# First recurrence of a two-block layer stack: where its values are turned, where its state products stand, and its low score levels issued in pairs

## The chip, the cores and the metric

The kernel runs on one core of a Trainium2 chip. The metric is the device time of one execution in microseconds (us), median of several executions; less is better. A core has a matrix engine (PE in the profile), a vector engine (DVE), an activation engine (ACT), a general engine (POOL) and an engine that issues the loads here (SP). Each runs its own list of instructions in order; they wait for each other through semaphores. PE writes only to PSUM, eight banks of 128 partitions x 512 float32.

## The reference, cut to what matters

The program is an attention layer, a gated recurrence with its projections, and a second block (a delta rule, a gated linear attention), for 2048 tokens of width 1024 in float32. The change is within the first recurrence alone, with 8 heads whose keys and values are 128 wide:

```
proj = h @ w_in;  q, f, i, z = split(proj)      # 4 x 1024 columns
q = silu(q);  k = 1 - exp(log_f);  v = i        # log_f: a log gate made of f
b = cumsum(log_f)                               # in a chunk
scores[t, s] = sum_k q[t] * exp(b[t] - b[s]) * k[s]        (s <= t)
o = (q * exp(b)) @ S + scores @ v
S = S * exp(b_last) + (k * exp(b_last - b)).T @ v
o = rmsnorm(o) * gnorm_w * silu(z)
```

## The kernel before, in words

`recurrence` (line 1017 of the profile's file) keeps features on the partitions and works in 32 units: a unit is one head and 512 tokens (four chunks of 128). Units 2n and 2n+1 are one visit: one head, two neighbouring groups of tokens, with the same weights. The visits pass the 8 heads over the first 1024 tokens and then over the second.

**Front of a unit.** Four projections, in the order q, z, f, v, each with eight steps (one per 128 rows of the contraction). A step is `product` (lines 191 to 195): three matmuls 128x128x512 of rounded parts, high by high, high by low, low by high. So a front has 32 steps and 96 matmuls. ACT then makes tanh of q, z and f and a logarithm (thq, thz, thf, lg), DVE makes q, z, k and the running sum b (lines 182, 178, 1423), and ACT takes v out of PSUM (step "v"). PE turns v, four 128x128 transposes ("vt", line 1138), and ACT copies the result to v_at. POOL makes the differences for score level 0 ("d", lines 1356 and 1357), ACT their exponential ("dx"), DVE its two halves e1 and e2 (lines 1437 and 1438); I call these two E0.

**Back of a unit.** Scores inside a chunk are made by halving. PE makes the diagonal ("diag", line 1152), then for levels 0 to 6 a product of keys with queries (steps "l0" to "l6"; line 1174 for levels 0 to 5, whose outputs are 64 partitions high, line 1170 for level 6). For each level from 1 on POOL makes differences, ACT exponentials ("dx1" ...), DVE two halves ("lev1" here for the two instructions of level 1, and so on); after PE, DVE merges the result into the scores (line 1466, "s0" ...). Then PE turns the keys ("kt", line 1184), DVE copies them out (line 1471), PE multiplies turned keys by turned values ("ds", line 1195), DVE carries four states (line 182, "st0" to "st3"), and PE makes the outputs in two halves ("o", lines 1205 and 1209). ACT squares the output ("sq"), PE sums over features ("norm", line 1219), ACT takes logarithm and exponential ("ln", "rs"), and DVE scales twice (line 1487 "on", line 182 "out").

**The order of the work** is written out by hand. Front and back are generators on each engine; `in_turn` runs front(u+1) and back(u) together, and `merge` (line 156) always advances the generator that is behind by its share of steps. The two counts are the numbers of `yield` in each:

```
merge((front(u + 1) if u + 1 < UN else None, 36), (back(u), 23))
```

A `yield` with nothing before it therefore only moves what follows later against the other generator. Of such a merge I say that its front is odd or even, by the number u+1.

**Weights.** SP loads the four weight blocks of the next visit (512 KB each, line 1097) as soon as the last products with the old ones are done. ACT rounds a block (128x1024, line 187) and POOL subtracts (line 1345). The code names them by the projection behind which they stand (`piece_due`): in fronts of odd units w(z), w(f), w(v) behind the projections z, f and v (they carry the weights of q, z and f of the next visit), in fronts of even units w(q), with the weights of v.

**PSUM.** The front has a ring of four banks, the back another, each taken in PE's order; who takes a bank waits until the one of four takes before has been read.

**Heads that begin.** In fronts of units 0, 1, 16 and 17 ACT and DVE also make the high and low parts of h (eight steps, line 1414), for which PE's q products wait.

Of the kernel before, what the change touches and what calls it, by code (L numbers as in the profile page):

```python
# [14 lines left out]
P = 128  # L15
# [19 lines left out]
LEVELS = 7  # L35
# [981 lines left out]
def recurrence(k):  # L1017
# [36 lines left out]
    set_a = k.steps("bounds_exp", "l0", "l1")  # L1054
    Fpe = k.steps("front_products", "q", "z", "f", "v", "vt")
    Fa = k.steps("front_scalar", "thq", "thz", "thf", "lg", "v", "dx", "vt")
    Fv = k.steps("front_vector", "q", "z", "k", "b", "e1", "e2")
    Fp = k.steps("front_pool", "d")
    Bpe = k.steps("back_products", "diag", *(f"l{l}" for l in range(LEVELS)), "kt", "ds", "o", "norm")
    Ba = k.steps("back_scalar", *(f"dx{l}" for l in range(1, 6)), "dx6", "eb", "dk", "sq", "ln", "rs")  # L1060
    Bv = k.steps("back_vector", "e1_1", "e2_1", "diag", *(x for l in range(5) for x in (f"e1_{l + 2}", f"e2_{l + 2}", f"s{l}")),
# [3 lines left out]
    def taken_front(kind, u):  # L1065
        at = {"q": (Fv, "q"), "z": (Fv, "z"), "f": (Fa, "thf"), "v": (Fa, "v"), "vt": (Fa, "vt")}
        s, name = at[kind]
        return s.by(name, u)

    def taken_back(kind, u):  # L1070
        at = {"diag": (Bv, "diag"), "kt": (Bv, "kt"), "ds": (Bv, "st3"), "o": (Bv, "on"), "norm": (Ba, "ln")}
        s, name = at[kind] if kind in at else (Bv, kind)
        return s.by(name, u)

    def in_turn(front, back):
        run(front(0))
        for u in range(UN):
            merge((front(u + 1) if u + 1 < UN else None, 36), (back(u), 23))

# [25 lines left out]
    def on_pe():  # L1105
# [16 lines left out]
        def front(u):  # L1122
            yield from project(0, "q", u)
            yield
            yield from project(3, "z", u)
            yield
            yield from project(1, "f", u)
            for _ in range(4):
                yield
            yield from project(2, "v", u)  # L1130
            yield
            b, before = fb.take("vt", u)
            pe.wait_ge(*Fa.by("v", u))
            if before is not None:
                pe.wait_ge(*taken_front(*before))
            for j in range(4):
                sl = slice(j * P, (j + 1) * P)
                ins = pe.transpose(b[:, sl], th(u, 2)[:, sl], k.c("ident"))
            ins.then_inc(*Fpe.did("vt"))
            yield  # L1140

        def back(u):
# [10 lines left out]
            ins.then_inc(*Bpe.did("diag"))  # L1153
            yield
            for l in range(LEVELS):
                H = 1 << l
                if l <= 5:
                    yield
                e = e0_at if l == 0 else e_of(u, l - 1)
                b, before = kb.take(f"s{l}", u)  # L1160
                if l == 0:
                    pe.wait_ge(*Fv.by("e2", u))
                else:
                    pe.wait_ge(*Bv.by(f"e2_{l}", u))
                if before is not None:
                    pe.wait_ge(*taken_back(*before))
                for i in range(4 if H == CH else 8):
                    if H == CH:
                        sl = slice(i * P, (i + 1) * P)
                        ins = pe.matmul(b[:, i * CH:(i + 1) * CH], e[:, sl], view(e[:, sl], H)[:, :, 1, :],  # L1170
                                        start=True, stop=True)
                    else:
                        own, sl = slice(i % 2 * CH, (i % 2 + 1) * CH), slice(i * CH, (i + 1) * CH)
                        ins = pe.matmul(b[own, i * CH // 2:(i + 1) * CH // 2], e[:, sl], view(e[:, sl], H)[:, :, 1, :],  # L1174
                                        start=True, stop=True)
                ins.then_inc(*Bpe.did(f"l{l}"))
                yield
            b, before = kb.take("kt", u)
# [6 lines left out]
            ins.then_inc(*Bpe.did("kt"))  # L1185
            yield
            yield
            b, before = kb.take("ds", u)
            pe.wait_ge(*Bv.by("kt", u))
            pe.wait_ge(*Fa.by("vt", u))  # L1190
            if before is not None:
# [4 lines left out]
            ins.then_inc(*Bpe.did("ds"))  # L1196
            yield
            b, before = kb.take("o", u)
# [48 lines left out]
    def on_act():  # L1247
# [10 lines left out]
        def front(u):  # L1258
            h, g = unit(u)
            if h == 0:  # L1260
                if g == 0:
                    a.wait_ge(*set_v.by("sel"))
                if u:
                    a.wait_ge(*Fpe.by("v", u - 1))
                for c in range(KC):
                    act(a, hi_of(g)[:, c, :], k.hT[:, c, cols(g)], ACT.Copy).then_inc(*h_a.did("hi"))
            yield from project("q", u)
            yield
            yield from project("z", u)
            yield  # L1270
            yield from project("f", u)
            a.wait_ge(*Fpe.by("z", u))
            if u:
                a.wait_ge(*Fv.by("z", u - 1))
            k.tanh(th(u, 0), fb.at("q", u), scale=0.5).then_inc(*Fa.did("thq"))
            if u:
                a.wait_ge(*Fpe.by("vt", u - 1))
            k.tanh(th(u, 1), fb.at("z", u), scale=0.5).then_inc(*Fa.did("thz"))
            a.wait_ge(*Fpe.by("f", u))
            if u:  # L1280
                a.wait_ge(*Fv.by("b", u - 1))
            else:
                a.wait_ge(*set_v.by("ab"))
            k.tanh(tf_at, fb.at("f", u), scale=0.5).then_inc(*Fa.did("thf"))
            a.wait_ge(*Fa.by("thf", u))
            k.ln(lg_at, tf_at, bias=ab[:, h:h + 1], scale=bb[:, h:h + 1]).then_inc(*Fa.did("lg"))
            for _ in range(4):
                yield
            yield from project("v", u)
            a.wait_ge(*Fv.by("q", u))  # L1290
            a.wait_ge(*Fpe.by("v", u))
            act(a, th(u, 2), fb.at("v", u), ACT.Copy).then_inc(*Fa.did("v"))
            a.wait_ge(*Fp.by("d", u))
            act(a, e0_at, e0_at, ACT.Exp).then_inc(*Fa.did("dx"))
            yield
            a.wait_ge(*Fpe.by("vt", u))
            act(a, v_at[u % 2], fb.at("vt", u), ACT.Copy).then_inc(*Fa.did("vt"))
            yield
# [5 lines left out]
        def back(u):  # L1304
            h, g = unit(u)
            level(u, 1)
            yield
            yield
            for l in range(LEVELS):
                if l + 2 < LEVELS:  # L1310
                    level(u, l + 2)
                    yield
                elif l + 2 == LEVELS:
                    if u:
                        a.wait_ge(*Bv.by("st3", u - 1))
                    act(a, eb_at, b_at[u % 2], ACT.Exp).then_inc(*Ba.did("eb"))
                    a.wait_ge(*Bp.by("dk", u))
                    act(a, d_of(u, 6), d_of(u, 6), ACT.Exp).then_inc(*Ba.did("dk"))
                    yield
                yield  # L1320
            for _ in range(5):
                yield
# [18 lines left out]
    def on_pool():  # L1341
# [17 lines left out]
        def front(u):  # L1359
# [4 lines left out]
            yield from project("f", u)  # L1364
            for _ in range(4):
                yield
            yield from project("v", u)
# [3 lines left out]
            differences(u, 0, e0_at).then_inc(*Fp.did("d"))  # L1371
            yield
            yield
# [12 lines left out]
        def back(u):  # L1386
            level(u, 1)
            yield
            yield
            for l in range(LEVELS):  # L1390
                if l + 2 < LEVELS:
# [7 lines left out]
                yield  # L1399
            for _ in range(8):  # L1400
                yield
# [5 lines left out]
    def on_dve():  # L1407
        def front(u):
# [7 lines left out]
            for _ in range(7 + 1 + 7 + 1 + 7 + 3):  # L1416
# [7 lines left out]
                                 op0=ALU.mult, op1=ALU.add).then_inc(*Fv.did("b"))  # L1424
            yield
            for _ in range(7):
                yield
            v.wait_ge(*Fa.by("dx", u))
            v.wait_ge(*Fv.by("k", u))
            halves(u, 0, e0_at, e0_at, Fv, "e1", "e2")  # L1430
            yield
            yield
# [11 lines left out]
        def back(u):  # L1444
# [4 lines left out]
            v.wait_ge(*Bpe.by("diag", u))  # L1449
            v.tensor_tensor(v4(sc_at), v4(kb.at("diag", u)), bc(k.c("ident"), 1, 4), ALU.mult).then_inc(*Bv.did("diag"))  # L1450
            yield
            for l in range(LEVELS):
# [18 lines left out]
            v.tensor_copy(kt_at, kb.at("kt", u)).then_inc(*Bv.did("kt"))  # L1471
            yield
            yield
            bs = kb.at("ds", u)
            v.wait_ge(*Bpe.by("ds", u))
            for j in range(4):
# [5 lines left out]
                else:  # L1482
                    stt(v, new, old, eb_at[:, j * P + P - 1:j * P + P], bs[:, sl], ALU.mult, ALU.add).then_inc(*Bv.did(f"st{j}"))
            for _ in range(5):
                yield
# [1295 lines left out]
```

## Time and profile before

| | us |
|---|---|
| median of 3 executions | 4064.3 |
| lowest, highest | 4064.14, 4067.91 |
| the profiled execution | 4071.8 |
| its span in the profile | 4070.5 |

The profile holds the start and duration of each instruction. A matmul's record is longer than the distance to the next one, since matmuls overlap: two products stand 0.23 us apart and have 0.39 us each. So I read costs on PE from the distance of starts. In a timeline a row's number in brackets is how long the engine had stood idle, and who released it; a row with x16 holds sixteen records; a float32 matmul leaves two.

### The profile page before, as it was taken

How to read it: one execution, taken by the hardware profiler on the slowest of the kernel's cores; microseconds unless marked ns; L12 is line 12 of the kernel's file. 1: busy time of each engine (PE TensorE's matmuls, PEld its weight loads, DVE VectorE, ACT ScalarE, POOL GpSimd, SP SyncE). 2: the span in 40 equal slices, each digit the busy share in tenths (PEclk: the TensorE clock that was granted, in tenths of full speed). 3: DMA queues.
4: the chain of work that ended last, by engine and by line, in shares of the span. 5: the costliest groups of instructions: out<-in, count | busy, mean ns of one | idle time of the engine just before them, and what ended most of it. 6: DMA issues, size and time to landing. Idle time of an engine off the chain costs nothing.

```text
span 4070.5 us, 78395 instructions
## 1 busy us (share of the span) xinstructions
PE 3683.8 (90%) x32928; PEld 2775.6 (68%) x32928; DVE 2043.2 (50%) x4568; ACT 1582.1 (39%) x2978; POOL 1124.8 (28%) x1214
## 2 busy tenths in 40 slices
PE   7999979897999998999997979999999996888889
PEld 4555548685777776777775856777776774777767
DVE  4655652344555555555554434656666664233222
ACT  2444441222344444443443324444444442344332
POOL 0000001132344443444432323222222320333232
PEclk9999989898999999999997989999999997999999
DMA  3000000122010110110101332111111113222132
GB/s 120 27 1 1 1 11 26 73 88 95 22 37 27 31 33 22 33 31 27 37 21 68 127 125 53 39 38 38 44 39 38 38 29 120 63 63 63 44 110 90
DMA packets 220093, 202.64 MB, mean 50 GB/s; under 512 B 7072, under 2 KB 191840, under 8 KB 219744
## 3 DMA queue, kind: packets, MB, share of 16 engines
q1 hardware_dynamic: 219744, 197.62, 15.5%
q8 instruction: 264, 4.33, 0.4%
q14 instruction: 85, 0.70, 0.1%
HBM read 164.04 MB, written 33.55 MB: 49 GB/s over the span
## 4 chain that ended last, share of the span: by engine, by line
PE 77%; DVE 10%; ACT 7%; issue 3%; DMA 2%; POOL 2%; SPq 1%; ACTq 0%; DVEq 0%; POOLq 0%
PE bank L193 18%; PE bank L195 16%; PE bank L194 16%; PE bank L447 4%; ACT arena L187 3%; PE bank L1174 3%; PE bank L2234 2%; DVE arena L685 2%; PE bank L2245 1%; ACT L277 1%; DVE arena L178 1%; PE bank L487 1%; ACT arena L188 1%; DVE arena L182 1%; PE bank L311 1%
## 5 line engine op out<-in xcount | busy, mean ns | idle before, releaser
L194 PE MATMUL bank<-hT_cut,arena_cut 128*128 128x512 f32 x2080 | 830.1, 399 | 0.0
L187 ACT ACTIVATE arena<-bank 128x512 f32<-128x512 f32 (+1 forms) x584 | 311.6, 570 | 745.2 <-PE bank L195 550.6
L193 PE MATMUL bank<-hT_cut,arena_cut 128*128 128x512 f32 x1112 | 515.7, 464 | 38.3 <-POOL arena_cut L1870 27.9
L187 ACT ACTIVATE arena<-arena 128x512 f32<-128x512 f32 (+3 forms) x690 | 359.4, 549 | 298.4 <-POOL arena L1357 222.4
L194 PEld LDWEIGHTS bank<-hT_cut,arena_cut 128*128 128x128 f32 x2080 | 401.5, 193 | 81.4 <-issue 19.0
L195 PE MATMUL bank<-hT_cut,arena_cut 128*128 128x512 f32 x1112 | 444.6, 400 | 0.0
L193 PE MATMUL bank<-arena_cut,hT_cut 128*128 128x512 f32 (+1 forms) x960 | 363.9, 379 | 61.7 <-POOL oT_cut L949 61.7
L188 ACT ACTIVATE arena<-arena 128x256 f32<-128x256 f32 (+2 forms) x336 | 210.1, 626 | 512.7 <-DVE arena L177 277.9
L193 PE MATMUL bank<-oT_cut,arena_cut 128*128 128x512 f32 x712 | 318.8, 448 | 56.9 <-POOL arena_cut L2503 23.0
L194 PE MATMUL bank<-arena_cut,hT_cut 128*128 128x512 f32 (+1 forms) x960 | 359.8, 375 | 0.0
L2503 POOL TENSOR_TENSOR arena_cut<-arena,arena_cut 128x256 fp32r<-128x256 f32 x272 | 224.3, 854 | 472.5 <-ACT arena_cut L187 472.4
L195 PE MATMUL bank<-arena_cut,oT_cut 128*128 128x512 f32 x768 | 306.1, 399 | 0.0
L447 PE MATMUL bank<-arena,hT 128*128 128x512 f32 (+1 forms) x768 | 297.0, 531 | 1.7 <-DVE arena L634 1.6
L193 PEld LDWEIGHTS bank<-hT_cut,arena_cut 128*128 128x128 f32 x1112 | 214.1, 193 | 106.0 <-ACT arena L187 30.3
L195 PE MATMUL bank<-oT_cut,arena_cut 128*128 128x512 f32 x712 | 283.6, 398 | 0.0
L1437 DVE TENSOR_TENSOR arena<-arena 128x256 f32<-128x256 f32 x224 | 149.4, 667 | 260.8 <-ACT arena L187 260.8
L187 ACT ACTIVATE arena<-bank,arena 128x512 f32<-128x512 f32 (+1 forms) x176 | 93.2, 561 | 468.2 <-PE bank L195 442.5
L187 ACT ACTIVATE arena_cut<-arena 128x1024 fp32r<-128x1024 f32 (+1 forms) x204 | 220.5, 1085 | 132.3 <-DMA arena<-in_rec_w_in 75.9
L1356 POOL TENSOR_TENSOR arena<-arena 128x256 f32<-128x256 f32 x224 | 146.7, 655 | 384.3 <-DVE arena L1423 254.5
L193 PEld LDWEIGHTS bank<-arena_cut,hT_cut 128*128 128x128 f32 x960 | 182.5, 190 | 99.2 <-issue 65.0
L195 PEld LDWEIGHTS bank<-hT_cut,arena_cut 128*128 128x128 f32 x1112 | 213.7, 192 | 50.3
L1345 POOL TENSOR_TENSOR arena_cut<-arena,arena_cut 128x1024 fp32r<-128x1024 f32 x64 | 155.4, 2430 | 302.4 <-ACT arena_cut L187 302.4
(237 smaller groups left out, 7079.3 us busy)
## 6 DMA issues: line engine op xcount, KB each, us to landing
arena<-in_w_in SPq DMA_DIRECT2D x100, 512.0 KB, 3.8
arena<-in_rec_w_in SPq DMA_DIRECT2D x64, 512.0 KB, 4.1
x_after<-arena SPq DMA_DIRECT2D x32, 512.0 KB, 2.6
arena<-x_after SPq DMA_DIRECT2D x32, 512.0 KB, 4.2
oT<-in_x SPq DMA_DIRECT2D x16, 512.0 KB, 3.4
arena<-in_x SPq DMA_DIRECT2D x16, 512.0 KB, 3.4
h_after<-hT SPq DMA_DIRECT2D x4, 2048.0 KB, 7.7
hT<-h_after SPq DMA_DIRECT2D x4, 2048.0 KB, 16.7
```

Of the source, the lines that this page charges most:

```text
L187: return e.activation(out, a, f, bias=bias, scale=scale)
L188: return e.activation(out, a, f, bias=bias, scale=scale, accum_out=accum)
L193: pe.matmul(out, a[0], b[0], start=start, stop=False)
L194: pe.matmul(out, a[0], b[1], start=False, stop=False)
L195: return pe.matmul(out, a[1], b[0], start=False, stop=stop)
L447: ins = pe.matmul(b[:, 0:n], k.hT[:, c, t * P:(t + 1) * P], wq[:, c, c0:c0 + n], start=(c == 0), stop=(c == KC - 1))
L685: m = v.tensor_tensor_reduce(out=prob4(u)[:, h, lo:], in0=banks.at(f"s{par}", u)[:, j * 256 + lo:(j + 1) * 256], in1=band[:, lo:], scale=H ...
L1174: ins = pe.matmul(b[own, i * CH // 2:(i + 1) * CH // 2], e[:, sl], view(e[:, sl], H)[:, :, 1, :], start=True, stop=True)
L1345: pool.tensor_tensor(w_lo[i], raw[i], w_hi[i], ALU.subtract).then_inc(*w_p[i].did("lo"))
L1356: pool.tensor_tensor(d4[:, :, 0, :], ref, b4[:, :, 0, :], ALU.subtract)
L1437: v.tensor_tensor(e4[:, :, 0, :], d4[:, :, 0, :], view(k_at[u % 2], H)[:, :, 0, :], ALU.mult).then_inc(*s.did(first))
L2503: ins = pool.tensor_tensor(w_lo[n % 3][:, c:c + 2, :], raw[n % 3][:, c:c + 2, :], w_hi[n % 3][:, c:c + 2, :], ALU.subtract)
```

## The change

The transposes of v leave the front and stand in the back behind the diagonal, with ACT's copy behind the exponential of level 2. Levels 0 and 1, 2 and 3, 4 and 5 are issued back to back on PE. Between kt and ds, and between ds and o, there are more steps of the other generator. Three idle steps of the front between f and v go, and the counts of the merge become 32 and 28. No arithmetic changes. The pieces of the diff below stand in this order: the names of the steps, the merge, PE's front, PE's back, ACT's front, ACT's back.

```diff
-    Fpe = k.steps("front_products", "q", "z", "f", "v", "vt")
-    Fa = k.steps("front_scalar", "thq", "thz", "thf", "lg", "v", "dx", "vt")
+    Fpe = k.steps("front_products", "q", "z", "f", "v")
+    Fa = k.steps("front_scalar", "thq", "thz", "thf", "lg", "v", "dx")
-    Bpe = k.steps("back_products", "diag", *(f"l{l}" for l in range(LEVELS)), "kt", "ds", "o", "norm")
+    Bpe = k.steps("back_products", "diag", "vt", *(f"l{l}" for l in range(LEVELS)), "kt", "ds", "o", "norm")
...
-            merge((front(u + 1) if u + 1 < UN else None, 36), (back(u), 23))
+            merge((front(u + 1) if u + 1 < UN else None, 32), (back(u), 28))
...
             yield from project(1, "f", u)
-            for _ in range(4):
-                yield
+            yield
             yield from project(2, "v", u)
-            yield
-            b, before = fb.take("vt", u)
-            pe.wait_ge(*Fa.by("v", u))
-            if before is not None:
-                pe.wait_ge(*taken_front(*before))
-            for j in range(4):
-                sl = slice(j * P, (j + 1) * P)
-                ins = pe.transpose(b[:, sl], th(u, 2)[:, sl], k.c("ident"))
-            ins.then_inc(*Fpe.did("vt"))
             yield
...
             ins.then_inc(*Bpe.did("diag"))
             yield
+            b, before = kb.take("vt", u)
+            pe.wait_ge(*Fa.by("v", u))
+            if before is not None:
+                pe.wait_ge(*taken_back(*before))
+            for j in range(4):
+                sl = slice(j * P, (j + 1) * P)
+                ins = pe.transpose(b[:, sl], th(u, 2)[:, sl], k.c("ident"))
+            ins.then_inc(*Bpe.did("vt"))
+            yield
             for l in range(LEVELS):
                 H = 1 << l
-                if l <= 5:
+                if l in (0, 2, 4):
+                    yield
                     yield
...
                 ins.then_inc(*Bpe.did(f"l{l}"))
-                yield
+                if l in (1, 3, 5):
+                    yield
+                    yield
+            yield
             b, before = kb.take("kt", u)
...
             ins.then_inc(*Bpe.did("kt"))
-            yield
-            yield
+            for _ in range(4):
+                yield
             b, before = kb.take("ds", u)
             pe.wait_ge(*Bv.by("kt", u))
-            pe.wait_ge(*Fa.by("vt", u))
+            pe.wait_ge(*Ba.by("vt", u))
...
             ins.then_inc(*Bpe.did("ds"))
-            yield
+            for _ in range(3):
+                yield
             b, before = kb.take("o", u)
...
-            for _ in range(4):
-                yield
+            yield
             yield from project("v", u)
...
             act(a, e0_at, e0_at, ACT.Exp).then_inc(*Fa.did("dx"))
             yield
-            a.wait_ge(*Fpe.by("vt", u))
-            act(a, v_at[u % 2], fb.at("vt", u), ACT.Copy).then_inc(*Fa.did("vt"))
-            yield
...
             for l in range(LEVELS):
                 if l + 2 < LEVELS:
                     level(u, l + 2)
                     yield
+                    if l == 0:
+                        a.wait_ge(*Bpe.by("vt", u))
+                        act(a, v_at[u % 2], kb.at("vt", u), ACT.Copy).then_inc(*Ba.did("vt"))
...
-            for _ in range(5):
+            for _ in range(9):
                 yield
             a.wait_ge(*Bpe.by("o", u))
```

The generators of POOL and DVE change in their `yield` alone: POOL's back has one more behind level 1 and 12 for 8 at its end; DVE's back one more behind the diagonal, 4 for 2 behind kt and 7 for 5 behind the states; the fronts of both lose four.

## Rows read from the trace of the kernel before

**Rows 1.** The page: busy time, share of the span and instructions of each engine

```profile
PE 3683.8 (90%) x32928; PEld 2775.6 (68%) x32928; DVE 2043.2 (50%) x4568; ACT 1582.1 (39%) x2978; POOL 1124.8 (28%) x1214
```

**Rows 2.** Windows: stretch, length, then PE, PEld, DVE, ACT, POOL busy, clock, DMA

```profile
1048.80:2132.50 1083.70, 1017.23 (x7485) 784.30 (x7485) 607.02 (x1069) 464.11 (x678) 463.37 (x509) 0.99 0.11 30
1740.50:1776.10 35.60, 33.73 (x252) 26.04 (x250) 21.53 (x35) 14.42 (x23) 15.60 (x20) 1.00 0.06 16
```

**Rows 3.** Groups by line, PE, 1040 to 2200 us: busy, mean, idle before

```profile
L1174 PE MATMUL bank<-arena 128*64 128x32 f32 x3072 | 128.5, 227 | 5.6 <-DVE arena L1438 5.6
L1209 PE MATMUL bank<-arena 128*128 128x128 f32 x240 | 50.5, 293 | 11.9 <-DVE arena L182 7.8 <-DVE arena L1481 4.1
L1195 PE MATMUL bank<-arena 128*128 128x128 f32 x256 | 38.0, 293 | 25.1 <-DVE arena L1471 25.1
L1138 PE MATMUL bank<-common_table,arena 128*128 128x128 f32 x128 | 21.0, 286 | 24.2 <-ACT arena L187 24.2
```

**Rows 4.** Timeline of PE (start, us, what): a low level between two products

```profile
1744.63 0.40 PE L195 MATMUL bank<-hT_cut,arena_cut 128*128 128x512 f32 x1
1744.95 0.66 PE L1174 MATMUL bank<-arena 128*64 128x32 f32 x16
...
1745.88 0.40 PE L194 MATMUL bank<-hT_cut,arena_cut 128*128 128x512 f32 x1
```

**Rows 5.** Timeline of PE: product, kt and ds (not shown), second product behind them

```profile
1763.39 0.40 PE L195 MATMUL bank<-hT_cut,arena_cut 128*128 128x512 f32 x1
...
1766.24 0.40 PE L194 MATMUL bank<-hT_cut,arena_cut 128*128 128x512 f32 x1
```

**Rows 6.** Timeline of PE: products around the first and the second half of the outputs

```profile
1767.16 0.39 PE L195 MATMUL bank<-hT_cut,arena_cut 128*128 128x512 f32 x1
...
1769.12 0.40 PE L194 MATMUL bank<-hT_cut,arena_cut 128*128 128x512 f32 x1
1769.36 0.39 PE L195 MATMUL bank<-hT_cut,arena_cut 128*128 128x512 f32 x1
...
1770.71 0.40 PE L194 MATMUL bank<-hT_cut,arena_cut 128*128 128x512 f32 x1
```

**Rows 7.** Timeline of PE: last product of a front, vt, next front's second product

```profile
1774.58 0.39 PE L195 MATMUL bank<-hT_cut,arena_cut 128*128 128x512 f32 x1
1775.72 0.66 PE L1138 MATMUL bank<-common_table,arena 128*128 128x128 f32 x4 [0.75 <-ACT arena L187]
...
1776.44 0.40 PE L194 MATMUL bank<-hT_cut,arena_cut 128*128 128x512 f32 x1
```

**Rows 8.** Timeline of ACT: w(v), ln, rs of one merge, sq of the next

```profile
1735.54 1.05 ACT L187 ACTIVATE arena_cut<-arena 128x1024 fp32r<-128x1024 f32 x1
...
1740.76 0.67 ACT L187 ACTIVATE arena<-bank,eps 128x512 f32<-128x512 f32 x1
1741.46 0.63 ACT L187 ACTIVATE arena<-arena 128x512 f32<-128x512 f32 x1
...
1770.68 0.60 ACT L187 ACTIVATE arena<-bank 128x512 f32<-128x512 f32 x1 [4.13 <-PE bank L1209]
```

**Rows 9.** Timeline of POOL: w(v), second half of level 0's differences, w(q)

```profile
1736.67 2.38 POOL L1345 TENSOR_TENSOR arena_cut<-arena,arena_cut 128x1024 fp32r<-128x1024 f32 x1 [8.94 <-ACT arena_cut L187]
...
1739.58 0.61 POOL L1357 TENSOR_TENSOR arena<-arena 128x256 f32<-128x256 f32 x1
...
1746.44 2.44 POOL L1345 TENSOR_TENSOR arena_cut<-arena,arena_cut 128x1024 fp32r<-128x1024 f32 x1 [1.69 <-ACT arena_cut L187]
```

**Rows 10.** Timeline of DVE: E0's two instructions, out, then one of level 3

```profile
1740.89 0.73 DVE L1437 TENSOR_TENSOR arena<-arena 128x256 f32<-128x256 f32 x1 [6.86 <-ACT arena L187]
1741.54 0.83 DVE L1438 TENSOR_TENSOR arena<-arena 128x256 f32<-128x256 f32 x1
...
1743.01 1.22 DVE L182 SCALAR_TENSOR_TENSOR oT<-arena 128x512 f32<-128x512 f32 x1
...
1747.09 2.08 DVE L1437 TENSOR_TENSOR arena<-arena 128x256 f32<-128x256 f32 x1
```

More of the change, by code:

```diff
@@ L1054, in recurrence @@
     set_a = k.steps("bounds_exp", "l0", "l1")
-    Fpe = k.steps("front_products", "q", "z", "f", "v", "vt")
-    Fa = k.steps("front_scalar", "thq", "thz", "thf", "lg", "v", "dx", "vt")
+    Fpe = k.steps("front_products", "q", "z", "f", "v")
+    Fa = k.steps("front_scalar", "thq", "thz", "thf", "lg", "v", "dx")
     Fv = k.steps("front_vector", "q", "z", "k", "b", "e1", "e2")
     Fp = k.steps("front_pool", "d")
-    Bpe = k.steps("back_products", "diag", *(f"l{l}" for l in range(LEVELS)), "kt", "ds", "o", "norm")
-    Ba = k.steps("back_scalar", *(f"dx{l}" for l in range(1, 6)), "dx6", "eb", "dk", "sq", "ln", "rs")
+    Bpe = k.steps("back_products", "diag", "vt", *(f"l{l}" for l in range(LEVELS)), "kt", "ds", "o", "norm")
+    Ba = k.steps("back_scalar", "dx1", "dx2", "vt", *(f"dx{l}" for l in range(3, 7)), "eb", "dk", "sq", "ln", "rs")
     Bv = k.steps("back_vector", "e1_1", "e2_1", "diag", *(x for l in range(5) for x in (f"e1_{l + 2}", f"e2_{l + 2}", f"s{l}")),
@@ L1065, in taken_front @@
     def taken_front(kind, u):
-        at = {"q": (Fv, "q"), "z": (Fv, "z"), "f": (Fa, "thf"), "v": (Fa, "v"), "vt": (Fa, "vt")}
+        at = {"q": (Fv, "q"), "z": (Fv, "z"), "f": (Fa, "thf"), "v": (Fa, "v")}
         s, name = at[kind]
@@ L1070, in taken_back @@
     def taken_back(kind, u):
-        at = {"diag": (Bv, "diag"), "kt": (Bv, "kt"), "ds": (Bv, "st3"), "o": (Bv, "on"), "norm": (Ba, "ln")}
+        at = {"diag": (Bv, "diag"), "vt": (Ba, "vt"), "kt": (Bv, "kt"), "ds": (Bv, "st3"), "o": (Bv, "on"), "norm": (Ba, "ln")}
         s, name = at[kind] if kind in at else (Bv, kind)
@@ L1276, in front @@
             if u:
-                a.wait_ge(*Fpe.by("vt", u - 1))
+                a.wait_ge(*Bpe.by("vt", u - 1))
             k.tanh(th(u, 1), fb.at("z", u), scale=0.5).then_inc(*Fa.did("thz"))
@@ L1308, in back @@
             yield
+            yield
             for l in range(LEVELS):
@@ L1364, in front @@
             yield from project("f", u)
-            for _ in range(4):
-                yield
+            yield
             yield from project("v", u)
@@ L1371, in front @@
             differences(u, 0, e0_at).then_inc(*Fp.did("d"))
-            yield
             yield
@@ L1389, in back @@
             yield
+            yield
             for l in range(LEVELS):
@@ L1399, in back @@
                 yield
-            for _ in range(8):
+            for _ in range(12):
                 yield
@@ L1424, in front @@
                                  op0=ALU.mult, op1=ALU.add).then_inc(*Fv.did("b"))
-            yield
-            for _ in range(7):
+            for _ in range(5):
                 yield
@@ L1430, in front @@
             halves(u, 0, e0_at, e0_at, Fv, "e1", "e2")
-            yield
             yield
@@ L1450, in back @@
             v.tensor_tensor(v4(sc_at), v4(kb.at("diag", u)), bc(k.c("ident"), 1, 4), ALU.mult).then_inc(*Bv.did("diag"))
+            yield
             yield
@@ L1471, in back @@
             v.tensor_copy(kt_at, kb.at("kt", u)).then_inc(*Bv.did("kt"))
-            yield
-            yield
+            for _ in range(4):
+                yield
             bs = kb.at("ds", u)
@@ L1483, in back @@
                     stt(v, new, old, eb_at[:, j * P + P - 1:j * P + P], bs[:, sl], ALU.mult, ALU.add).then_inc(*Bv.did(f"st{j}"))
-            for _ in range(5):
+            for _ in range(7):
                 yield
```

## The prediction, made before the changed kernel ran

> **What bounds the kernel now.** I first read the page [rows 1]: PE is busy 90% of the span, the next engine 50%, so anything that leaves PE's list or PE's waits counts at once, as long as PE stays last. Next the windows of the stage [rows 2]: over 30 merges PE is busy 1017 of 1084 us at clock 0.99, DVE 607, ACT 464, POOL 463. A plain merge lasts 35.6 us (there PE 33.7, DVE 21.5, ACT 14.4, POOL 15.6). No other engine is near its limit; only latency could replace PE. Then the groups by line for PE's idle time [rows 3]: three places hold most of it, ds behind DVE's copy of the keys (25.1 us), vt behind ACT's step v (24.2), the outputs behind the states (11.9). Last the timeline, for what it costs PE to leave the products and come back. A change smaller than 0.2% (8 us) can't be told from none.
>
> **Costs on PE, from distances of starts.** Two products are 0.23 apart [rows 6], a step of three 0.69. I take an insertion's cost as the distance from the product before it to the second product after it, less 0.46.
> - A low level [rows 4]: 1745.88 - 1744.63 - 0.46 = 0.79. Its sixteen records last 0.66, one of them 0.23 [rows 3], so they start over 0.43 us, 0.029 apart; the other 0.33 is the way in and out.
> - kt with ds [rows 5]: 2.85 - 0.46 = 2.39, of it 25.1 / 32 = 0.78 idle behind the copy [rows 3].
> - Half of the outputs, eight records of 128x128 [rows 6]: the second half 1.35 - 0.46 = 0.89, the first, which waits for states, 1.96 - 0.46 = 1.50. ds alone has the form of the second.
> - vt [rows 7]: 1.86 - 0.46 = 1.40. From its own start to the second product is 0.72; with a 0.23 lead in place of the wait that is 0.49. kt is four transposes too.
>
> **Part by part, per merge.**
> 1. *Pairs.* The second level of a pair needs no way in and out: it adds 0.46 in place of 0.79, and 0.33 is saved three times, 1.0. No row has two low levels in a row. Bounds: 0 if a level pays its way whatever stands before it, 0.33 if all of it goes; below nothing is excluded, as no record is added. I take 0.33, since in the second half of the outputs two kinds of product alternate and all eight records fit in 0.89 [rows 6].
> 2. *vt behind the diagonal.* 1.40 becomes 0.49, 0.9 saved, if v is out of PSUM by then. It is: the old vt, which waits for just that, starts 1.14 us behind the last product [rows 7]; the new one has three more product steps and the diagonal before it, some 2.9 us. ACT's copy of vt (0.6 us) now stands in front of dx3; ds, its only reader, comes 19 us later. The back's ring has 13 takes for 12; each predecessor is read at least 2 us before its bank is wanted.
> 3. *kt and ds apart.* PE now issues f2, kt, f3 to f6, ds. Cost 0.49 + 0.89 = 1.38 for 2.39, 1.0 saved. Cover: four steps of 0.69 = 2.8 us; DVE's copy needed 0.78 beyond kt's own time.
> 4. *ds and o apart.* Four steps stand between them for two, and DVE's states come before q, z, k, b in its list instead of behind them (kt, st0 to st3, q, z, k, b). Then the first half costs what the second does: 0.89 for 1.50, 0.6 saved ([rows 3] shows 11.9 us of idle time, part of it). q, z, k, b start behind the states, but lg, for which k waits, is later anyway.
> 5. *The three empty steps* cost nothing themselves, they only set the order.
>
> Sum 1.0 + 0.9 + 1.0 + 0.6 = 3.5 per merge: 35.6 becomes 32.1, if nothing becomes late.
>
> **What becomes late.** I wrote out the orders of both merges from the `yield` counts. The new one on PE is q0 q1 diag q2 vt q3 q4 q5 l0 l1 q6 q7 z0-z2 l2 l3 z3-z6 l4 l5 z7 f0 f1 l6 f2 kt f3-f6 ds f7 v0-v2 o v3 o v4 v5 norm v6 v7. On ACT the tail was sq w(v) v dx ln rs vt; it is now sq **ln rs w(v)** v dx. On POOL d0 stands behind w(v), on DVE E0 now behind on and out. So in merges with an odd front, w(v) waits for norm. With t = 0 at the next merge's first product:
> - norm starts at -(1.38 + 0.87) = -2.25. PE to ACT takes 1.1 (sq starts at 1770.68, its output half began 0.23 behind 1769.36) [rows 6, 8], so ln starts at -1.15, rs 0.70 later, w(v) at about 0.2 [rows 8].
> - POOL's w(v) starts 1.13 later, 1.3 [rows 8, 9]; d0 ends 3.52 later, 4.8 [rows 9]; E0 ends 2.18 later, 7.0 [rows 9, 10].
> - l0 is due at 6 x 0.69 + 0.8 (the diagonal, sixteen records like a low level) + 0.49 + 0.1 = 5.6. PE waits 1.4. Behind it stand all products.
> - l1 is due 0.46 behind l0. lev1 follows E0 on DVE and has two instructions as E0 has (1.48 us in [rows 10]), so it ends at 8.4. Delay so far 2.35.
> - l5: POOL makes d1 to d3 by 8.9 (two instructions of 0.61 each [rows 9], up to 1.5 a pair where DVE's reads fall on them, an estimate after the 0.73 and 0.83 of [rows 10]), dx3 ends at 9.6 (0.63 as rs), w(q) is rounded by 10.7 and subtracted by 13.2 (2.44) [rows 9], d4 and d5 end at 16.1, dx5 at 16.8, lev5 at 18.1. Due 14.75 + 2.35 = 17.1, wait 1.0. l3 just passes: lev3 ends at 11.1, as w(q) starts.
>
> So a merge with an even front (15 of the 31) gives back about 3.3 and lasts 35.4; one with an odd front (16) has no w(v) before its d0, and E0 waits only for on and out: out ended 2.77 behind rs's start [rows 8, 10], so at 2.3 now; E0 ends by 3.8 and lev1 by 5.3, both in time for 5.6 and 6.05. It lasts 32.1. There dx6 and dk also move in front of w(z) on ACT and POOL, so they come earlier.
>
> The bounds of the give-back: 0 if the chain from norm runs 3.3 us quicker than these rows add up to, 4.9 if w(q) also gets hold of lev3. [Rows 10] shows that case: an instruction of level 3 took 2.08 us while w(q) ran, where E0's second took 0.83; l3 would then wait 0.9 more, l5 0.7.
>
> The Trainium skill, page "SBUF — State Buffer", section "Who interferes with whom", makes the DVE-POOL collision an exclusive lock: whoever starts first holds the read port for the whole instruction. By it lev3 is free or 2.4 us late, nothing between. The 2.08 us agree. With the lock lost in every even-front merge the sum would be 15 x 1.6 = 24 us more, 4033.
>
> **Sum.** 16 x 3.5 + 15 x 0.2 = 59. The merge before unit 16 gains nothing, since its q products wait for ACT's high parts behind the later dx: -3.5. Total 55.5. The profiled execution is 4071.8, 7.5 above the median; against it 4016.3, against the median 4064.3 - 55.5 = **4008.8**. Span and execution differ by 1.3 only, so I don't correct for it.
>
> **Rivals.**
> - *A, nothing becomes late* (or little). 31 x 3.5 = 108, 3956; half the give-back 3984. For it: slack in DVE, ACT and POOL [rows 2]. Against: w(v) can't start before rs, whatever the slack. 0.20 for the stretch 3956 to 3990, little of it at the end.
> - *B, the pairs don't pay*: each level pays its way in and out. In odd-front merges 1.0 less, in even-front ones less of the waiting: 16 to 31 us fewer, 4025 to 4040. For it: no row shows a pair. 0.10.
> - *C, slower: POOL's weight subtractions sit on the path.* Four per two merges, w(z), w(f), w(v), w(q), 2.4 us each [rows 9]. Now only w(v) and w(q) reach PE. If DVE's level work stood behind each of the four for its whole length, two merges would lose 9.8 and gain 7.0: +2.8 x 15.5 = 43, 4107. It decides from 7.0 us per two merges, nearly three of the four. For it [rows 10]; against, w(z) and w(f) now run behind dk, when DVE only has qt, dk and the merges of scores. 0.04.
> - *D, no difference*: E0 late in odd-front merges too (over 5.6 + 3.5 there). It has 1.8 us of cover before l0 waits at all. 0.04.
>
> My forecast, give-back 2.3 to 5, has 0.62 (of it 0.15 for lev3 held up by w(q), 4033). **Range:** 3974 (give-back 1.0: 15 x 2.3 = 35 less) to 4036 (give-back 4.9 is 4033, and most of B). That leaves out A's end, C, D and the last of B. Faster 0.92, same 0.03, slower 0.05.
>
> **What would show it.** Merges alternate, 32.1 and 35.4 us (distance of the norm records of successive units). In the merge with an even front, l0 idle for 1.4 behind E0, l1 for 0.9 behind DVE's line 1438, l5 for 1.0. w(v) on ACT right behind rs. A pair holds 32 records and costs 1.25. No idle time at vt, ds and o. The forecast is wrong if both kinds of merge last the same, if a pair costs 1.58, or if l0 never waits.

## The result, and the profile after

The changed kernel takes 4024.5 us (median of 4, 4018.65 to 4027.93), the kernel before 4064.2 beside it; the ratio is 0.990, 95% interval 0.9882 to 0.9917. So it is 40 us faster, where I had forecast 55 (4008.8, range 3974 to 4036). Its profiled execution took 4018.65 with a span of 4017.4; it lies 5.9 below its median, and that of before lay 7.6 above its own. Between the two traces I therefore compare the stage alone: from the first product of the recurrence to its last output, 1177.3 us before (1017.3 to 2194.6) and 1130.3 after (1016.8 to 2147.1). That is 47.0 us less.

Windows of the changed kernel, columns as in [rows 2]: the long stretch, then a merge with an odd front, one with an even front, and 3.4 us within the latter.

```profile
1048.80:2089.50 1040.70, 990.71 (x7479) 801.40 (x7479) 580.91 (x1066) 468.48 (x673) 461.27 (x508) 0.97 0.11 31
1882.60:1914.60 32.00, 32.00 (x252) 26.03 (x251) 18.55 (x35) 15.42 (x23) 11.57 (x12) 1.00 0.18 50
1914.60:1951.10 36.50, 33.80 (x252) 27.31 (x251) 19.44 (x35) 15.41 (x23) 19.25 (x23) 0.95 0.05 16
1924.00:1927.40 3.40, 3.40 (x16) 2.72 (x15) 2.56 (x7) 1.57 (x2) 1.76 (x1) 0.54 0.02 5
```

Every plain merge (one without the waits of a beginning head) had 35.6 before [rows 2]. Now the odd ones last 31.8 to 32.0, with PE busy throughout, and the even ones 36.5 or 36.6, three of them 37.6 to 37.9. **The even-front merges are slower than before the change**; the odd ones pay for all.

Groups of PE between 1040 and 2150 us, columns as in [rows 3]:

```profile
L1174 PE MATMUL bank<-arena 128*64 128x32 f32 x3072 | 115.4, 228 | 42.2 <-DVE arena L1439 42.2
L1213 PE MATMUL bank<-arena 128*128 128x128 f32 x240 | 47.2, 279 | 0.0
L1198 PE MATMUL bank<-arena 128*128 128x128 f32 x256 | 34.7, 279 | 0.8 <-DVE arena L1473 0.8
L1151 PE MATMUL bank<-common_table,arena 128*128 128x128 f32 x128 | 19.2, 272 | 0.1
```

The three waits of [rows 3] are gone: the outputs (now L1213) from 11.9 to 0, ds (L1198) from 25.1 to 0.8, vt (L1151) from 24.2 to 0.1. In their place the low levels wait 42.2 us for the second of DVE's two halves (L1439), 5.6 before. So 60.3 us of waiting went and 36.6 came.

PE in an even-front merge, start and duration. First the last product ahead of level 0, then levels 0 and 1, no longer in one row because PE waits between them, and the products behind:

```profile
1919.74 0.39 PE L195 MATMUL bank<-hT_cut,arena_cut 128*128 128x512 f32 x1
1921.86 0.66 PE L1174 MATMUL bank<-arena 128*64 128x32 f32 x16 [1.73 <-DVE arena L1439]
1923.49 0.93 PE L1174 MATMUL bank<-arena 128*64 128x32 f32 x16 [0.97 <-DVE arena L1439]
1924.34 0.80 PE L193 MATMUL bank<-hT_cut,arena_cut 128*128 128x512 f32 x1
1924.94 0.63 PE L194 MATMUL bank<-hT_cut,arena_cut 128*128 128x512 f32 x1
1925.37 0.63 PE L195 MATMUL bank<-hT_cut,arena_cut 128*128 128x512 f32 x1
...
1928.94 0.40 PE L195 MATMUL bank<-hT_cut,arena_cut 128*128 128x512 f32 x1
1929.27 1.12 PE L1174 MATMUL bank<-arena 128*64 128x32 f32 x32
...
1930.66 0.40 PE L194 MATMUL bank<-hT_cut,arena_cut 128*128 128x512 f32 x1
```

By distances, level 0 starts 1.79 late (it stands 2.12 behind the product, where 0.33 is usual) and level 1 another 1.16 (1.63 behind level 0, where 0.47 is usual). Then the products stand 0.43 apart and take 0.63 each, instead of 0.23 and 0.39: TensorE's clock is at its lower level, 1.2 GHz, from 1923.7 to 1927.1. The pair at 1929.27 is clean: 1930.66 - 1928.94 - 0.46 = 1.26.

The chain ahead of level 0: ACT's ln, rs, w(v); POOL's w(v), second half of d0, and later w(q); DVE's second halves of E0 and of level 1.

```profile
1913.38 0.69 ACT L187 ACTIVATE arena<-bank,eps 128x512 f32<-128x512 f32 x1 [1.66 <-PE bank L1223]
1914.10 0.63 ACT L187 ACTIVATE arena<-arena 128x512 f32<-128x512 f32 x1
1914.64 1.04 ACT L187 ACTIVATE arena_cut<-arena 128x1024 fp32r<-128x1024 f32 x1
```

```profile
1915.76 2.72 POOL L1349 TENSOR_TENSOR arena_cut<-arena,arena_cut 128x1024 fp32r<-128x1024 f32 x1 [9.40 <-ACT arena_cut L187]
...
1919.02 0.60 POOL L1361 TENSOR_TENSOR arena<-arena 128x256 f32<-128x256 f32 x1
...
1925.64 2.53 POOL L1349 TENSOR_TENSOR arena_cut<-arena,arena_cut 128x1024 fp32r<-128x1024 f32 x1 [1.69 <-ACT arena_cut L187]
```

```profile
1920.97 0.83 DVE L1439 TENSOR_TENSOR arena<-arena 128x256 f32<-128x256 f32 x1
...
1922.59 0.83 DVE L1439 TENSOR_TENSOR arena<-arena 128x256 f32<-128x256 f32 x1
```

w(v) starts as rs ends. The second half of E0 ends at 1921.80 and level 0 starts 0.06 later; level 1's halves end at 1923.42, and level 1 starts 0.07 later.

### The profile page after: what moved, and what is told of

Same layout as the page of the kernel before. It is cut to its first block, busy times and chain, and to the rows that moved or that the text cites. A ratio compares the mean times of both kernels' runs of the same rounds, so it can differ in the third digit from the quotient of the medians.

```text
span 4017.4 us, 78395 instructions
## 1 busy us (share of the span) xinstructions
PE 3652.9 (91%) x32928; PEld 2788.0 (69%) x32928; DVE 2016.4 (50%) x4568; ACT 1588.5 (40%) x2978; POOL 1122.8 (28%) x1214
## 4 chain that ended last, share of the span: by engine, by line
PE 72%; DVE 10%; issue 6%; ACT 5%; POOL 4%; DMA 3%; SPq 1%; DVEq 0%; POOLq 0%; ACTq 0%
PE bank L193 17%; PE bank L195 15%; PE bank L194 15%; PE bank L447 4%; PE bank L1174 2%; POOL arena_cut L1349 2%; ACT arena L187 2%; PE bank L2236 2%; DMA arena<-in_rec_w_in 2%; DVE arena L685 2%; PE bank L2247 1%; PE bank L487 1%; ACT arena L188 1%; PE bank L311 1%; ACT arena_cut L187 1%
## 5 line engine op out<-in xcount | busy, mean ns | idle before, releaser
L194 PEld LDWEIGHTS bank<-hT_cut,arena_cut 128*128 128x128 f32 x2080 | 407.3, 196 | 85.3 <-issue 19.0
L193 PEld LDWEIGHTS bank<-hT_cut,arena_cut 128*128 128x128 f32 x1112 | 216.5, 195 | 109.5 <-ACT arena L187 30.3
L195 PEld LDWEIGHTS bank<-hT_cut,arena_cut 128*128 128x128 f32 x1112 | 215.9, 194 | 50.8
L447 PEld LDWEIGHTS bank<-arena,hT 128*128 128x128 f32 x768 | 139.2, 191 | 116.7 <-issue 108.6
```

The lines of the kernel that those rows point to most:

```text
L193: pe.matmul(out, a[0], b[0], start=start, stop=False)
L194: pe.matmul(out, a[0], b[1], start=False, stop=False)
L195: return pe.matmul(out, a[1], b[0], start=False, stop=stop)
L447: ins = pe.matmul(b[:, 0:n], k.hT[:, c, t * P:(t + 1) * P], wq[:, c, c0:c0 + n], start=(c == 0), stop=(c == KC - 1))
```

## The experiments

**Theory 1:** what even-front merges give back comes from w(v) behind norm, and behind it from w(q) and the clock. **Rivals:** the pairs don't pay; the level chain can't feed pairs; the low clock is a cost of its own. All times below are medians of 4 executions (e4: 10); the kernel before took 4065.8 to 4066.4 beside them.

**e1, w(v) one step earlier on ACT** (between sq and ln).

```diff
-            yield from project("v", u)
+            for _ in range(KC - 2):
+                yield
+            split(*piece_due(u, "v"))
+            yield
             a.wait_ge(*Fv.by("q", u))
```

> The changed kernel, with the rounding of w(v) on ACT one front step earlier, so that it stands between sq and ln instead of behind rs; nothing else. Theory 1 (w(v) behind norm makes level 0 late, and all that the even-front merges give back follows from that): POOL's w(v) starts about 30.3 us into the odd-front merge instead of 33.2, E0 ends before l0 is due, no wait at l0 and l1, TensorE's clock stays at its upper level there, and even-front merges last about 32.0 as the odd ones do: 15 x 4.5 = 68 us less than the changed kernel, about 3957. Rival (the even-front merges are held by POOL's w(q) on DVE and POOL, or by the clock whatever l0 does): they stay above 35 us, 4010 or more.

3975.4 us, ratio 0.978 (0.9764 to 0.9797), 49 us less than the changed kernel; the stage lasts 1085.9 for 1130.3, 44 less. Levels 0 and 1 wait no more, but I had expected 3957: the even-front merges last 33.4, three of them 35.0, not 32.0. Windows of an even-front merge, an odd-front one and one of the three long ones, then PE at levels 4 and 5:

```profile
1682.00:1715.50 33.50, 32.34 (x252) 26.25 (x251) 19.49 (x35) 14.63 (x22) 17.61 (x23) 1.00 0.06 17
1715.50:1747.50 32.00, 32.00 (x252) 26.04 (x251) 18.59 (x35) 16.36 (x24) 13.41 (x13) 1.00 0.18 50
1747.50:1782.50 35.00, 33.83 (x252) 27.30 (x250) 19.50 (x35) 14.55 (x22) 17.52 (x23) 0.95 0.06 16
```

```profile
1696.30 0.66 PE L1174 MATMUL bank<-arena 128*64 128x32 f32 x16
1698.12 0.66 PE L1174 MATMUL bank<-arena 128*64 128x32 f32 x16 [1.17 <-DVE arena L1442]
```

Level 5 is 1.36 late (1.82 behind level 4 for 0.46). That is the third wait of the forecast (1.0), which the changed kernel doesn't show. Where the clock then fell for 3.4 us, the merge lasted 1.6 more (35.03 for 33.45 by the distance of the norm records).

**e2, w(v) between ln and rs**, that is 0.5 us earlier.

```diff
...
             k.ln(d_of(u, 7), ...).then_inc(*Ba.did("ln"))
+            if u + 1 < UN:
+                split(*piece_due(u + 1, "v"))
```

The piece left out takes the rounding from its old place behind rs.

> The changed kernel, with the rounding of w(v) on ACT between ln and rs, one instruction (0.7 us) earlier and not more. Theory 1: E0 ends 0.7 to 0.9 us earlier, l0 waits 0.8 instead of 1.7, l1 as before 0.9. Two outcomes are told apart by it: if TensorE's clock still falls in even-front merges, they last about 35.7 (15 x 0.8 = 12 us less in all, about 4012); if the shorter wait keeps the clock up, the products behind l1 run at 0.69 a step, l5 waits up to 1.0, and the merges last 33.7 to 34.7, about 3990.

4012.8 us (0.9869, 0.9854 to 0.9884). Level 0 waits 1.25, level 1 1.16, in every even-front merge. Eight of the fourteen plain ones kept the full clock and lasted 35.8 all the same, since level 5 then waited 1.36: 32.0 + 1.25 + 1.16 + 1.36 = 35.8. In four the clock fell for 3.4 us, from 8.4 to 9.9 us into the merge on, level 5 waited nothing, and they lasted 35.9 or 36.0. In two it fell for 6.8: 37.3. Windows of one of the first kind and one of the last:

```profile
1633.00:1668.80 35.80, 32.50 (x252) 26.21 (x251) 20.43 (x35) 15.29 (x23) 19.37 (x23) 1.00 0.06 16
1700.80:1738.10 37.30, 35.15 (x251) 28.34 (x250) 20.52 (x35) 15.27 (x23) 19.32 (x23) 0.91 0.06 15
```

So 3.4 us of low clock behind level 1 cost little of their own, 0.1 to 0.2: they take the place of level 5's wait. I had expected 33.7 to 34.7 with the clock up and 35.7 with it down; both kinds lasted 35.8 to 36.0.

**e3, no pairs**: PE's six low levels one by one, a `yield` ahead of and behind each.

> The changed kernel with the six low levels issued one by one, each with one empty step ahead and one behind; the counts of the merge are kept at 32 and 28. By the way in and out of 0.33 us per insertion, odd-front merges last 1.0 longer (32.9 instead of 31.9) and show no wait. In even-front merges l0 comes earlier in PE's order and waits more, l1 waits less, so they change by -0.5 to +1.0. In all 10 to 30 us more than the changed kernel. Rival (a pair saves nothing, the gain is all from the waits): the odd-front merges stay at 31.9.

4040.9 us (0.9937, 0.9922 to 0.9952), 16 more than the changed kernel. Odd-front merges last 32.8 to 33.0, exactly 1.0 more. In the even-front ones PE stands idle for 2.43 ahead of level 0; the six that kept the full clock last 35.9, the other eight 37.0 to 38.4. The pairs are worth their 1.0 where PE is the last. The window of an odd-front merge:

```profile
1684.10:1717.10 33.00, 33.00 (x251) 26.06 (x250) 19.42 (x35) 15.43 (x23) 11.61 (x12) 1.00 0.17 49
```

**e4, ds at kt**: the four `yield`s between kt and ds moved behind ds.

> The changed kernel with ds right behind kt again, and all seven empty steps behind ds, so that o keeps its place. PE then waits for DVE's copy of the turned keys: each merge 1.0 us longer (odd-front 32.9, even-front 37.5), 31 us in all, about 4055. Rival (the wait was covered by something else that becomes late, so that the place of ds is worth nothing): no change.

4066.0 us (0.9997, 0.9988 to 1.0006): 41 us more, not 31. The odd-front merges are 1.0 longer as expected. Of the 14 plain even-front ones, twelve last 38.6 to 39.0, 2.2 longer, and in these the clock was low for 6.8 us; in all it was low for 102 us of the merges (75 in the changed kernel). The window of one of the twelve:

```profile
1735.50:1774.50 39.00, 35.52 (x251) 28.47 (x250) 19.54 (x35) 15.40 (x23) 19.18 (x23) 0.91 0.05 14
```

The other two tell the parts from each other. In one the clock was low for 3.4 us, as in most of the changed kernel's, and it lasts 37.6, 1.0 longer than those. In one the clock kept its upper level in spite of the same waits at levels 0 and 1, level 5 waited 1.17 by its record, and it lasts 37.4.

**e5, e1 and the weights of v behind z**, so that in even fronts this split stands behind dk.

```diff
...
+        if u % 2 == 0:
+            return (2, u // 2) if after == "z" and u else (None, None)
...
```

> w(v) before ln as in e1, and in even fronts the rounding and subtraction of the weights of v behind z instead of behind q (so behind dk on ACT and POOL, as w(z) stands in odd fronts). In e1 the even-front merges lasted 33.4, of it 1.36 waiting at l5 for lev5, behind d4 and d5, behind POOL's w(q). If that is w(q)'s doing, l5 waits no more and even-front merges last 32.0 as odd ones; the clock, which fell in three of e1's merges, stays up. 15 x 1.4 + 3 x 1.6 = 26 us less than e1: about 3950. Rival (the level chain of POOL, ACT and DVE is itself too slow for l5 in pairs): l5 still waits 0.5 or more, 3960 to 3975.

3954.4 us (0.9721, 0.9706 to 0.9736). All plain merges last 31.8 to 32.1 with PE busy from end to end, the clock at its upper level:

```profile
1637.80:1669.80 32.00, 32.00 (x251) 26.04 (x250) 18.48 (x35) 16.36 (x24) 13.41 (x13) 1.00 0.18 50
1669.80:1701.90 32.10, 32.10 (x251) 26.12 (x250) 21.72 (x35) 14.61 (x22) 17.53 (x23) 1.00 0.06 18
```

The level chain can feed pairs.

**e6, the same move of v's weights alone**, w(v) left behind rs.

> The changed kernel with the weights of v behind z in even fronts, and w(v) left behind rs. In the changed kernel l5 never waits in the trace, because the stretch at the lower TensorE clock behind l1 gives lev5 the time. By that, taking w(q) away is worth nothing here though it is worth 1.4 a merge in e5: l0 waits 1.8, l1 1.2, the clock falls, even-front merges last 36.5, 4018 to 4028. Rival (w(q) also holds up lev1 to lev3, or the clock falls because of the whole sequence and not of l0 and l1 alone): even-front merges below 35.5, 4010 or less.

4017.0 us (0.9875, 0.9859 to 0.9891); even-front merges 36.5 and 36.6, three of 37.6 to 38.0, as in the changed kernel, the stage 1130.4 us for 1130.3:

```profile
1709.10:1745.70 36.60, 33.90 (x252) 27.28 (x251) 19.69 (x35) 15.46 (x23) 19.29 (x23) 0.95 0.05 15
```

What is worth 1.4 a merge in e5 is worth nothing here: level 5's wait lies under the slow stretch. The median is still 7.5 below the changed kernel's; by the stage, none of that is the edit's, so medians of 4 executions can lie that far apart.

**e7, pairs alone on the kernel before**, w(v) where it was.

> The kernel before with the pairs alone: only the yields around the levels of PE change, counts stay 36 and 23. With w(v) still ahead of v, dx and ln nothing gives the gain back: all merges 34.6 for 35.6 (three times 0.33 us), 31 us in all, about 4035. Rival (in pairs the second level comes too early for DVE even here, as w(q) delays lev5 in even fronts): even-front merges gain less than odd ones.

4035.9 us (0.9919, 0.9902 to 0.9937), 30 us less than before; both kinds of merge last 34.6:

```profile
1685.00:1719.70 34.70, 32.82 (x254) 26.12 (x252) 17.87 (x35) 16.01 (x24) 15.12 (x15) 1.00 0.17 47
1719.70:1754.30 34.60, 32.73 (x252) 26.02 (x251) 20.94 (x35) 14.41 (x23) 15.57 (x20) 1.00 0.06 16
```

**e8, vt alone on the kernel before.**

> The kernel before with the transposes of v behind the diagonal alone (front and back yields moved with them, rates 36 and 24, w(v) still ahead of ln on ACT). All merges 0.9 to 0.95 us shorter, 34.7, 28 to 29 us in all, about 4037. Rival (the wait moves on to l0, whose E0 is now due 1.4 us earlier against the front's end): less than 15 us.

4043.9 us (0.994, 0.9925 to 0.9955), 22 us less. Plain merges last 34.6 to 34.7 as expected, but this isn't a clean measure: with the rates 36 and 24 a product step slipped between kt and ds. PE's groups show it, ds's wait down from 25.1 to 3.3 and the outputs' grown from 11.9 to 33.1:

```profile
L1209 PE MATMUL bank<-arena 128*128 128x128 f32 x240 | 50.4, 292 | 33.1 <-DVE arena L182 23.6 <-DVE arena L1482 9.5
...
L1195 PE MATMUL bank<-arena 128*128 128x128 f32 x256 | 38.0, 293 | 3.3 <-DVE arena L1472 0.8
L1152 PE MATMUL bank<-common_table,arena 128*128 128x128 f32 x128 | 19.2, 273 | 0.4 <-ACT arena L187 0.4
```

The two cancel to 0.6 us in all, and vt's own cost by distances went from 1.40 to 0.45. The four merges where heads begin gained next to nothing (37.1, 40.6, 42.0, 37.3 for 37.4, 40.5, 41.4, 38.3), which makes 3 of the 7 us that are missing. The stage is 26.8 shorter (1150.5 for 1177.3); the rest lies outside it or in the difference of executions.

**e9, ds at kt in e5.**

> e5 with ds right behind kt and all seven empty steps behind ds. In e4, on the changed kernel, this cost 1.0 in odd-front and 2.2 in even-front merges; the profile puts the second 1.2 on TensorE's clock, which was low for 102 us of that stage in place of 75. In e5 no wait and no low clock is left, so by that account ds costs 1.0 in every merge: 32.9 to 33.0 for all, 31 us more than e5, about 3985. Rival (even-front merges pay more for this place of ds for a reason of their own): they last 34 or more, 4000.

3985.6 us (0.9798, 0.9781 to 0.9814), 31.2 more than e5. All plain merges 32.8 to 33.1. PE's waits there:

```profile
PE bank L1198 <- DVE arena L1476: 23.5, 30, 0.8
```

So in e4 the further 1.2 of the even-front merges belongs to their second 3.4 us of slow clock, not to ds, as the merge of 37.6 there says too.

**e10, the low levels in threes** on e5: four `yield`s ahead of level 0, five ahead of level 3, three behind level 5.

> e5 with the six low levels issued in threes, 0 to 2 behind z0 and 3 to 5 behind z6, instead of in pairs. One way in and out less, 0.33 a merge, 10 us in all, about 3944, if the third level of each three finds its halves ready: lev2 ends at 8.2 in even-front merges of e5 and l2 would be due at about 9, lev5 ends at 13.4 and l5 would be due at about 14.3. Rival (s0 to s2 come later, and DVE's list puts lev3 to lev5 behind them): l5 or l6 waits and the gain is gone, 3950 to 3965, and in even-front merges the clock may fall too.

3943.8 us (0.9697, 0.9682 to 0.9711), the fastest of all, 120 us less than the kernel before. Merges last 31.4 to 31.7, no level waits:

```profile
1632.30:1663.90 31.60, 31.60 (x251) 26.00 (x250) 20.54 (x35) 16.20 (x24) 13.64 (x13) 1.00 0.18 51
1663.90:1695.60 31.70, 31.70 (x252) 26.05 (x251) 22.37 (x35) 14.63 (x22) 17.68 (x23) 1.00 0.06 18
```

**e11, o near ds** on e5: one `yield` between them for three, two more behind o.

> e5 with one empty step between ds and o in place of three, and two more behind o; DVE's list stays, with the states ahead of q, z, k, b. If DVE's order is what freed o of its wait (0.6 a merge), o finds state 0 ready 1.2 us behind ds too and nothing changes: 3952 to 3958. Rival (the distance did it): the first half of o waits 0.3 to 0.6 a merge as before, 10 to 18 us more, about 3968.

3958.0 us (0.9727, 0.9712 to 0.9741); the stage lasts 1061.9 us for e5's 1061.5, and no output waits. Two steps of products stand between ds and o here, as many as in the kernel before, where the outputs waited. So the distance is worth nothing. What differs is DVE's list: before, DVE ran q, z, k and b between its copy of the keys and the states; here the states come first. No run turns that order alone, so it is the cause by elimination.

## Why the prediction was right, and where it was off

- **What PE is spared** held to a tenth. By the same distances as in the forecast: a pair 1.26 (1.25), vt 0.45 (0.49), kt 0.45 (0.49), ds 0.90 (0.89), each half of the outputs 0.90 (0.89). Odd-front merges last 31.8 to 32.0 for 32.1. e3 and e7 show the pairs' 1.0 each way, e9 the 1.0 of kt and ds. Rival B is out.
- **w(v) behind norm** was right in place and mechanism: e1 takes it away and 49 us with it. Its size was low: level 0 was 1.79 late for 1.4, level 1 1.16 for 0.95. POOL's w(v) took 2.72 for 2.38 and started with DVE's out, and level 1's halves had 1.70 from first start to end, for 1.48. My own terms also sum to a little more than I wrote: level 0 is due at 5.53, not 5.6, and lev1 ends at 8.48, not 8.4. Rival A is out.
- **Level 5 behind w(q)** is there, 1.36 for 1.0, but only where the clock keeps its upper level (e1, eight merges of e2, one of e4). In the changed kernel this step of the forecast failed: I had left TensorE's clock at its upper level. It fell in all 14 plain even-front merges, in eleven for 3.4 us behind the two waits, in three for 6.8 from between them on. Even-front merges last 32.1 in e5, so those 3.4 us took 36.55 - 32.1 - 1.79 - 1.16 = 1.5, in place of the 1.36. Against the 1.0 of the forecast this is 0.5 a merge: 0.36 because the wait was sized too low, 0.1 to 0.2 for the clock (e2 and e4 have merges of both kinds side by side, 35.8 with 36.0 and 37.4 with 37.6). It is 1.0 to 1.4 more in the three merges where the clock stayed low for 6.8 us. That the clock cost so little was luck: the slow stretch happened to lie where I had put a wait.
- **The sum**: the 14 plain even-front merges last 36.5 or 36.6 for 35.4, and three of them 1.0 to 1.4 more: 19 us short of the forecast. Plain odd-front ones are 0.2 better, 2 us. The merge before unit 16 gained 0.2, forecast 0; the other three where heads begin gained 4.0, 3.3 and 4.7, together 5 more than forecast; the front that runs alone at the start gained 2, the end of the stage 1 more than one merge. 55.5 - 19 + 2 + 5 + 2 + 1 = 46.5, the stage's 47.0. Between that and the 39.7 of the medians 7 us stay open: they lie outside the stage or in the difference of executions (e6 shows as much between equal stages).
- **Rival C** can be closed: of four weight subtractions two reached PE, and after their move (e5) none. lev3 did pass in front of w(q) (the second half began at 1925.52, w(q) at 1925.64), so the case of the lost lock, 4033, did not occur. Where w(v) began 0.27 behind DVE's out (0.75 long, from 1915.49), it took 2.72 for 2.38, and out's 0.75 is its shortest anywhere in the stage: DVE came first and POOL waited. That agrees in its order with the exclusive lock of the Trainium skill, page "SBUF — State Buffer", section "Who interferes with whom"; in size only roughly, as POOL lost 0.34 where out had 0.48 left to run.
- **o** gained its 0.6, but of my two reasons the distance was worth nothing (e11); DVE's order is what is left.

## What to carry to other kernels

When an edit shortens an in-order engine's list, write out the new order of the *other* engines as well and look for what has slipped behind a late result: here one rounding that slipped behind a logarithm cost more than the change kept (49 of the 89 us that are there once it is mended), and moving it one `yield` gave it back. A wait can lie under another loss: w(q) was worth 0 with w(v) late and 21 us without, so test such suspects again after each one that is mended. A group of float32 matmuls with 64-partition outputs in a stream of wide ones cost 0.33 us here for its way in and out together, with 16, 32 or 48 records in it (0.79, 1.26 and 1.73 by distances), so in this kernel they were best issued in few, large groups.

## What the runs showed that I had not expected

In the changed kernel TensorE's clock fell to 1.2 GHz though PE had never stood idle for more than 1.73 us at a stretch in a plain merge. The idle times below are those in the brackets of the rows. PE stood idle for 1.73 and 0.97, with 0.66 of work between them, in each of the 14 plain even-front merges. In eleven the clock fell behind both waits, for 3.4 us; in three it fell behind the first, ahead of level 1, for 6.8. The same two waits brought it down in 13 of 14 merges in e4, and 1.18 with 0.97 in 6 of 14 in e2. One wait alone did it too: 2.43 at level 0 in 8 of 14 (e3), 1.17 at level 5 in 3 of 14 (e1). The waits of each merge before, 0.75 at vt, 0.78 at ds and 0.34 to 0.51 at the outputs, did not bring it down in any plain merge [rows 2, 3], nor did 1.02 to 1.19 at the outputs in e8. So the same waits brought it down in one merge and not in another of the same run; which merges it takes stays open here.
